# In a mixture-of-experts loop, ScalarE copies the next weights ahead of scaling the finished expert's second half

## The reference

```python
out = jnp.zeros(hf.shape, jnp.float32)
for e in range(N_EXPERTS):                                       # 16
    y = (jax.nn.silu(h @ w_gate[e]) * (h @ w_up[e])) @ w_down[e]  # D 1024 -> 512 -> 1024
    out = out + combine[:, e:e + 1] * y.astype(jnp.float32)
```

## Time and profile before

| | |
|---|---|
| median of 3 runs | 589.69 us (589.64 to 591.5) |
| profiled execution | 592.38 us |
| its span | 590.5 us |
| busy share of the span | PE 95%, PEld 78%, DVE 71%, ACT 60%, POOL 20% |
| chain that ended last, by engine | PE 85%, DVE 6%, DMA 5% |
| expert part | from about 278 us to the end |

### The profile page before, as it was taken

The page is one execution under the profiler, slowest core; times in us unless marked ns, Lnnn a source line. Parts: engine busy times, 40 slices in busy tenths (PEclk is TensorE's granted clock), DMA queues, the critical chain, the costliest instruction groups (busy, mean ns, idle before and its releaser), DMA issues.

```text
span 590.5 us, 8063 instructions
## 1 busy us (share of the span) xinstructions
PE 562.8 (95%) x2773; PEld 460.6 (78%) x2774; DVE 422.1 (71%) x567; ACT 353.4 (60%) x471; POOL 115.3 (20%) x101
## 2 busy tenths in 40 slices
PE   4799999999999999998999999999999999999982
PEld 3688878888887888877888888888888888888860
DVE  2822565552684662466888998888998889988877
ACT  3713544586023344243687878888877878777723
POOL 4230000000000000002323344223444233411100
PEclk9999999999999999998999999999999999999997
DMA  8997222012201043799799999999999999994073
GB/s 294 383 327 278 72 72 72 2 70 73 72 19 53 2 159 130 256 318 344 276 350 375 365 370 383 369 372 358 374 379 386 372 373 370 362 388 146 21 286 142
DMA packets 72012, 144.84 MB, mean 245 GB/s; under 512 B 3778, under 2 KB 13162, under 8 KB 71856
## 3 DMA queue, kind: packets, MB, share of 16 engines
q1 hardware_dynamic: 65936, 125.49, 59.7%
q0 software_dynamic: 6048, 18.99, 9.4%
HBM read 133.29 MB, written 14.69 MB: 251 GB/s over the span
## 4 chain that ended last, share of the span: by engine, by line
PE 85%; DVE 6%; DMA 5%; issue 1%; ACT 1%; SPq 1%; POOLq 0%; DVEq 0%
PE ps L1262 24%; PE ps L1264 23%; PE ps L1263 23%; PE ps L1269 5%; DMA arena<-w_in 3%; PE ps L1334 2%; PE ps L1304 2%; DMA arena<-y_dram 2%; PE ps L1371 2%; PE ps L1359 1%; PE ps L1277 1%; PE ps L1402 1%; PE ps L1325 1%; DVE res L1249 1%; DVE act_lo L858 1%
## 5 line engine op out<-in xcount | busy, mean ns | idle before, releaser
L1062 DVE TENSOR_TENSOR lo_ring<-arena,hi_ring 128x2048 fp32r<-128x2048 f32 x94 | 215.1, 2291 | 30.2 <-ACT hi_ring L763 29.1
L1262 PE MATMUL ps<-hi_ring,act_hi 128*128 128x512 f32 x576 | 232.5, 404 | 0.2 <-DVE act_lo L858 0.2
L1264 PE MATMUL ps<-hi_ring,act_lo 128*128 128x512 f32 x576 | 225.2, 391 | 0.0
L1263 PE MATMUL ps<-lo_ring,act_hi 128*128 128x512 f32 x576 | 224.6, 390 | 0.0
L763 ACT ACTIVATE hi_ring<-arena 128x2048 fp32r<-128x2048 f32 x94 | 180.2, 1917 | 18.5 <-PE ps L1264 18.5
L1262 PEld LDWEIGHTS ps<-hi_ring,act_hi 128*128 128x128 f32 x576 | 108.2, 188 | 27.3 <-issue 6.0
L1264 PEld LDWEIGHTS ps<-hi_ring,act_lo 128*128 128x128 f32 x576 | 108.1, 188 | 23.5
L1263 PEld LDWEIGHTS ps<-lo_ring,act_hi 128*128 128x128 f32 x576 | 108.4, 188 | 20.1
L849 DVE TENSOR_TENSOR lo_ring<-arena,hi_ring 128x512 fp32r<-128x512 f32 x68 | 45.2, 687 | 45.9 <-ACT hi_ring L614 45.4
L858 DVE TENSOR_TENSOR act_lo<-ps,act_hi 128x512 fp32r<-128x512 f32 x64 | 41.5, 683 | 9.9 <-ACT act_hi L801 3.5
L545 POOL DMA_INDIRECT y_dram<-y,row_info x15 | 16.1, 1072 | 149.6 <-issue 149.6
(11 more groups left out here) (189 smaller groups left out, 532.3 us busy)
## 6 DMA issues: line engine op xcount, KB each, us to landing
arena<-w_gate SPq DMA_DIRECT2D x32, 1024.0 KB, 11.7
arena<-w_up SPq DMA_DIRECT2D x32, 1024.0 KB, 11.9
arena<-w_down SPq DMA_DIRECT2D x32, 1024.0 KB, 11.2
arena<-w_in SPq DMA_DIRECT2D x16, 512.0 KB, 8.2
y_dram<-arena POOLq DMA_DIRECT2D x8, 512.0 KB, 11.4
arena<-w_out SPq DMA_DIRECT2D x4, 1024.0 KB, 5.0
arena<-y_dram SPq DMA_DIRECT2D x8, 512.0 KB, 6.9
arena<-w_in SPq DMA_DIRECT2D x3, 1024.0 KB, 17.5
```

Of the source, the lines that this page charges most:

```text
L1062: nc.vector.tensor_tensor(lo(N1 + n12), raw(n12), hi(N1 + n12).bitcast(F32), ALU.subtract).then_inc(lo_done, 1)
L1262: nc.tensor.matmul(dst, a_hi, b_hi, start=start, stop=False)
L1263: nc.tensor.matmul(dst, a_hi, b_lo, start=False, stop=False)
L1264: return nc.tensor.matmul(dst, a_lo, b_hi, start=False, stop=stop)
```

## The change

The scaling of one half is put into a helper, `scale_half`. At the end of a step only the first half is scaled (both in the last step); the second half of expert e is scaled in the step of e + 1, behind its first high copy and ahead of the copy of the turned rows. No wait is added or taken away; the count waited for is written for the expert before.

```diff
+            def scale_half(b, a, done):
+                act.wait_ge(mm_done, done)
+                nc.scalar.activation(y_buf[b][:, a * 512:(a + 1) * 512], ps[:, 2 + a, :], ACT.Copy,
+                                     scale=row_info[:, 4 * b + 2:4 * b + 3].bitcast(F32)).then_inc(y_scaled, 1)
+
-            def step(b, e, q, last=False, first=False):
+            def step(b, e, q, last=False, first=False, later=True):
                 n = e * PER_E + 4
                 for c in range(2 if last else PER_E):
                     n12 = (4 + PER_E * b + c) % RING2
                     split(n + c, n12, q * 16 + 16 * (1 + (4 + PER_E * b + c) // RING2))
+                    if c == 0 and later:
+                        scale_half(1 - b, 1, e * PER_E + (used_value(N1 + 7) - PER_E))
                     if c == 0 and not last:
                         for a in range(2):
                             act.wait_ge(x_turned, e * 2 + 3 + a)
...
                 act.wait_ge(info_ready, e + 1)
-                for a in range(2):
-                    act.wait_ge(mm_done, e * PER_E + used_value(N1 + (4 if last else 6) + a))
-                    nc.scalar.activation(y_buf[b][:, a * 512:(a + 1) * 512], ps[:, 2 + a, :], ACT.Copy,
-                                         scale=row_info[:, 4 * b + 2:4 * b + 3].bitcast(F32)).then_inc(y_scaled, 1)
+                for a in range(2 if last else 1):
+                    scale_half(b, a, e * PER_E + used_value(N1 + (4 if last else 6) + a))
...
             for e in range(2):
-                step(e, e, 0, first=True)
+                step(e, e, 0, first=True, later=(e > 0))
```

## The result

| | before | after |
|---|---|---|
| median of 11 runs each | 589.69 us | 591.84 us |
| profiled execution, its span | 592.38, 590.5 | 590.8, 589.0 |
| first step's T0 (start of the turn) | 287.70 | 284.87 |
| mean step of the loop | 17.94 us | 17.91 us |
| last T0 (step 14) to the start of SP's read-back | 21.17 | 23.21 |

The changed kernel takes 1.0040 times as long, with a 95% interval from 1.0026 to 1.0053: slower by 1.5 to 3.1 us. The medians lie 2.15 us apart, 0.36%, where 1.7 us, 0.28%, were forecast. The spans of the two profiled executions say the opposite, since this one reached its first expert step 2.8 us earlier, before the change can act. So I compare stretches, each from a T0 of its own.

The account below looks back on a forecast made before the run. TensorE, busy 95% of the span, was taken to bound the kernel. A loop gain of 0.2 us and an end loss of 1.88 gave +1.7 on 589.69, 591.4 us, with a range of 589.4 to 592.3.

Parts of the forecast that it names:

- The swap itself: ScalarE, each step: copy starts at 392.82 instead of 393.41, scaling 0.1 before its end; the rows' high parts don't move.
- Term 1: Loop: 12 steps gain 0.01 to 0.02 us each, 0.2 us in all, bounds 0 and 0.6.
- the gate's 0.19: TensorE's stall of 0.19 us per loop step at the next expert's first gate product, expected to go.
- Rival (a): Loop: the whole stall is won, 12 x 0.19 = 2.3 us gained against 1.88 lost, 589.3 us; chance 0.07.
- Rival (d): Loop: TensorE's wait for hid answers as slowly as the gate's, 0.10 x 12 = 1.2 us lost, 592.8; chance 0.06.
- Term 2: End: the late scaling of expert 14's second half delays its scatter, 1.88 us lost, lower end 1.80.
- the 0.17 of the text: End: time the scatter of expert 14 was to stand at VectorE's low copy, 0.17 us.
- the 0.84 named as a sign: End: the scatter was to finish 0.84 us behind the end of a low copy.
- the danger: End: expert 14's scatter misses the gap between VectorE's last two low copies, +4.7 us, total 594.2; chance 0.07.
- The sum: Whole kernel: -0.2 + 1.88 = +1.7 us on 589.69, giving 591.4 us or +0.28%.
- a spread under 1 us: Condition on timing: runs of one kernel must spread under 1 us, or none of the signs can be told.
- Rival (e): ScalarE: the copy does not start before 393.4, nothing gained and 0.6 more lost at the end, 592.2; chance 0.05.

Follow-up runs that it names:

- the table of four: Mean loop steps with ScalarE's old and new order: 17.94 and 17.91 us with VectorE's second low copy whole, 17.95 and 17.75 with it in halves.
- end-only one: Against the changed kernel, old order in every step but one: only expert 14's second half is scaled behind step 15's first high copy; 591.43 us, ratio 1.0052.
- held scatter: Changed kernel with the scatter of expert 14 held until ScalarE's last high copy is done; one profiled execution, 593.56 us.
- the one with the waits alone: Kernel before with TensorE's x_lo wait put last of three ahead of the next expert's first gate product; 588.85 us, ratio 0.9979.
- halves kernel: Kernel before with VectorE's second low copy in two halves, hidden rows between, ScalarE's order old: 589.09 us, ratio 0.999; with x_lo last, 587.91 us.

## Why the prediction was right

**The swap itself** went as worked out: the copy at the place of the scaling, the scaling 0.1 before the copy's end, nothing moved behind it.

**Term 1, the loop.** Forecast 0.2 us won, bounds 0 and 0.6; the trace has 12 x 0.027 = 0.3. The step that carried it, that hid is next in line and takes the gate's 0.19 back, is shown by the table of four: the same early copy is worth 0.03 a step with hid late and 0.2 with hid early. Rival (a) needed the full 0.19 and is out. Rival (d) needed a turn of hid 0.22 behind L1192; in the changed kernel it is 398.85 - 398.80 = 0.05 behind it, as in the written-out steps.

**Term 2, the end.** Forecast 1.88 us lost; the read-back starts 2.04 later. The path is as worked out, and the sizes are off by little. The scatter starts 1.85 later against T0, not 1.80, since the copy starts 0.06 later behind TensorE than the scaling did (551.09 against T0 is 15.45, 554.21 against T0 was 15.39). For standing at the low copy the sum has 1.88 - 1.80 = 0.08 (the 0.17 of the text is the way to the low copy's end; a scatter that starts then still has 0.84 to go, not 0.93). Measured is 0.97 - 0.93 = 0.04: the scatter began 0.18 before the end of the low copy that ends at 555.33 and was done 0.79 behind it, near the 0.84 named as a sign. From there to the landing it took 0.15 more than before, which the sum had at nothing: the whole is 3.68 instead of 3.49. That 0.15 need not come from the change, since in the seven other kernels with the early scatter the landing took 3.60 to 3.64. They start the read-back 21.14 to 21.36 after the last T0, the changed kernel and the end-only one 23.21 and 23.22, so a late scatter costs 1.85 to 2.08. The held scatter shows that the danger was real and the gap wide enough.

**The sum.** -0.3 + 2.0 = +1.7 us by these stretches, as forecast (591.4); measured 591.84, inside the forecast's own range, with 1.5 to 3.1 us by the interval. The medians put the change at 0.36%, just beyond the 0.3% that I took as the bound and had at 0.28%: I gave 0.51 to no difference and 0.47 to slower, and it came out on the slower side. The 0.4 between 1.7 and 2.15 is within the interval. From the start of the read-back to the end of the span the three kernels with a late scatter took 29.75, 29.79 and 30.15; of those with the early one six took 28.58 to 29.33, but the one with the waits alone took 30.24 and the kernel before 30.51. So one profile of each shows no cost of a late scatter there. I had also asked for a spread under 1 us between runs of one kernel, or none of this could be told. It was 3.0 us before and 2.5 after, so single executions don't tell it; the interval over 11 of each and the stretches of the traces do.

**Rival (e)**, a copy that doesn't start early, is out by the timeline.

## What to carry to other kernels

Before a wait is shortened, compute when the next wait of the same engine would end if the first one were gone. Here TensorE would have reached the hidden rows within 0.1 us of their end, so both waits had to be moved, and each edit alone showed next to nothing. A change in a loop body is also a change in its last turn, where what was slack inside may be the head of the chain to the end: here the copy in front was free 14 times and cost 2 us the 15th, and keeping the old order for that one step, with the hidden rows between two halves of the low copy, gives 587.1 us, 2.4 us under the kernel before. Where an engine stands at several waits before one instruction, their order can count for 0.1 us and more: here the one that comes last, put at the end, won 0.13 in each step of the loop and lost 0.06 to 0.08 in the written-out ones (halves kernel), so read both in the trace.

## What the runs showed of the hardware

- The order of TensorE's waits ahead of one weight load matters. With x_lo, the last to come, first of three waits, the load started 0.21 to 0.27 us after the last subtraction in the loop and 0.05 to 0.06 after it in written-out steps; with x_lo last it was 0.05 to 0.06 in the loop and 0.11 to 0.12 in written-out steps. That the counts worked out from the loop's register cost the 0.21 is likely, but was not tested apart from the loop.
- A GpSimd indirect DMA that began 0.24 to 0.29 us inside a VectorE subtraction of two SBUF tensors took 2.84 to 2.86 us instead of 0.93 to 0.96 and ended 0.80 to 0.84 us behind it, in seven traces. One that began 0.18 us before such an end took 0.97 and ended 0.79 behind it, and one that began 0.02 us ahead of such a subtraction took 0.96.
- Two subtractions of 1024 columns cost 1.23 + 1.22 us against 2.29 for one of 2048; with the overlap of neighbours, about 0.08 us for a point at which other work can be put in.
